# A hybrid decoder layer on one core: token projections reordered with stores in two parts, and a recurrence with two levels as rectangles

## The chip, the cores and the metric

The kernel runs on one core of one Trainium2 chip. The metric is the device time in microseconds of one execution; lower is better. Line numbers (L1153) are those of the kernel before.

## What is computed

One layer of a decoder for 1024 prompt tokens and 32 sample tokens (8 sequences of 4), all fp32: a feed-forward block, a combined projection of the normed stream, two mixers fed by it (sparse attention with an indexer that picks keys, and a gated linear recurrence), a merge, and a second feed-forward block. Two pieces matter here.

```
q, k, v, qi, ki, wi, hq, hf, hi, hg, ga, gr = split(h @ w_in)
q, k = rope(rms_norm(q)), rope(rms_norm(k));  qi, ki = rope(qi), rope(ki);  wi *= IDX_HEADS ** -0.5
# recurrence, per head (4 heads, key and value width 128)
f = lb + (1 - lb) * sigmoid(hf);  k = (1 - lb) * sigmoid(-hf);  G = cumsum(log f) within a chunk
A[t,s] = sum_d q[t,d] * exp(G[t,d] - G[s,d]) * k[s,d]   for s <= t
o = (q * exp(G)) @ S + A @ v;   S = exp(G_last) * S + (k * exp(G_last - G)).T @ v
rec = rms_norm(o) * silu(hg)
```

The projections from h, the state S of the prompt and of each sample, and the keys and values are outputs too.

## The kernel before, in words

The stages follow one another on all engines: first feed-forward (to about 832 us), token projections (834 to 1050), indexer scores, key selection with the rest of the projection, attention, recurrence (1696 to 1906), merge, second feed-forward. Each engine has its own hand-written program per stage, tied to the others by semaphores; a stage ends when SP (the queue that issues the DMAs) has seen its stores land.

**token_projections (L965 to L1336).** The columns of w_in come in seven groups of 256 (CHUNKS, L930), the last, "qk", with 72 more columns: the indexer key and the head weights. Each group is run over nine token tiles, so there are 63 steps (STEPS, L934). A step is 24 matmuls on TensorE (eight slices of depth, each as hi\*hi + hi\*lo + lo\*hi, L1153 to L1155) into one of four PSUM slots; ScalarE takes the result to SBUF (`taken`, or `out` for "hv"). Of "q" and "k" groups ScalarE squares the rows and takes a root, and VectorE does the statistics, a Newton step, the norm and the rotation (`statistics`, `norm`, `finish`); "qi" has the rotation alone; "hv" has nothing but ScalarE's copy. `finish(m)` runs one turning step late, except for "qk", where it runs at once and does the 64-wide key and the weights too, from `ki_in`, a copy that ScalarE makes (L1200). TensorE turns (transposes) the rotated rows four steps later (three for "qk", L1042), ScalarE keeps them in `stage` (L1188, L1190), and SP stores each group's `stage` whole, once its ninth tile is kept. `stage` has two slots, so a third group waits for the store of the first. The order before is: "q", then "hv" and "q" in turn, "hv" and "k", "qi" between, and last nine steps of "qk" alone. The fp32 weights come in by DMA (LOAD_AT), ScalarE makes the high part (`hi`, SPLIT_AT) and VectorE the low part (`low`, LOW_AT); TensorE waits for w_lo_done at a group's first step. In the first steps VectorE's order is: norm of step 0, `tables_with(0)` (which waits for the cosine and sine tables' DMA), step 1, then low(1). SP also fetches 64 pages of indexer keys, two a step from step 9 on.

**recurrence (L2323 to L3133).** Four heads; each head has eight prompt tiles of 128 tokens and one samples' tile, worked off in two units (u = 0: tiles 0 to 3; u = 1: tiles 4 to 8). The 128x128 lower triangle A is cut by levels: for block size b of 64, 32, 16, 8, 4, 2, 1 the later half of every 2b block looks at the earlier half, and an eighth product is the diagonal. For a level VectorE makes distances, ScalarE their exp (`decays`), VectorE the queries `qL` (`queries`); TensorE multiplies all 128 keys with 64 queries (`pair_products`, L3011 to L3024), VectorE masks the two halves (`mask`, L2872), and TensorE multiplies each level's part with the values (`outputs`, L3068, L3070). Each fp32 matmul shows as two in the trace, so eight products are sixteen. The state runs beside it: `turn` transposes the keys `kd`, ScalarE copies them to kdT, `states` multiplies with hv, VectorE updates S. Between units TensorE does outputs of the last tile, `ready` (waits for all seven `qL` of the next unit), pair_products, turn, states. Per unit VectorE also does `forget` (f from the loaded sigmoid, L2795), the scan, the masks, `variance` (L2919) and `factor` (L2944); POOL does the other steps of the norm's root (`newton`, `refine`, `gated`), the middle of which waits for `factor`.

Of the kernel before, what the change touches and what calls it, by code (L numbers as in the profile page):

```python
# [29 lines left out]
P = 128  # L30
# [892 lines left out]
HD = 64  # L923
# [6 lines left out]
CHUNKS = [("q", 0, 0), ("hv", 2632, 0), ("q", 256, 2), ("hv", 2888, CW), ("k", 512, 0), ("qi", 1024, 0), ("qk", 1280, 2)]  # L930
# [34 lines left out]
def token_projections(nc, hhi, hlo, w_in, q_gain, k_gain, cos, sin, ident, qT_d, kT_d, qiT_d, kiT_d, wi_d, hv_d,  # L965
# [10 lines left out]
    KEEP_LATER = 5  # L976
    with Scope(nc, "tok") as s:
# [3 lines left out]
        sq_room = s.sb("sq", [P, 4 * KI_COLS])  # L981
        ki_in = sq_room[:, :].rearrange("p (a b) -> p a b", b=KI_COLS)
        sq = sq_room[:, 0:CW]
        ki_out = s.sb("ki_out", [P, 2, 2 * HD + HEADS])
        taken = s.sb("taken", [P, 4, CW])
# [17 lines left out]
        ki_stored = [s.sem(f"ki_stored{n}") for n in range(2)]  # L1003
        proj_done, take_done, sq_done = s.sem("proj_done"), s.sem("take_done"), s.sem("sq_done")
# [4 lines left out]
        stage_stored = [s.sem(f"stage_stored{n}") for n in range(2)]  # L1009
        block = s.block()  # L1010
# [14 lines left out]
        def weights(w, c):  # L1025
# [3 lines left out]
            place = (c + 2) % WS  # L1029
# [10 lines left out]
        def turn_later(m):  # L1040

            return m + (3 if kind(m) == "qk" else 4)  # L1042
# [15 lines left out]
        def _(sp):  # L1058
            def load(c):
                if c > 2:  # L1060
                    sp.wait_ge(w_lo_done, c - 2)
                at = CHUNKS[c][1]
                sp.dma_start(raw[c % 2], wv[:, :, at:at + CW]).then_inc(w_loaded[c % 2], 16)
                if kind_of(c) == "qk":
                    sp.wait_ge(w_lo_done, c - 1)
                    sp.dma_start(raw[(c + 1) % 2][:, :, 0:KI_COLS], wv[:, :, at + CW:at + QK]).then_inc(w_loaded[(c + 1) % 2], 16)

            def store_stage(m):
# [4 lines left out]
                sp.dma_start(dst[b:b + 2].rearrange("b p t -> p b t"), stage[:, at, :, :]).then_inc(stage_stored[at], 16)  # L1073
                if kind(m) == "qk":
                    sp.dma_start(kiT_d[0:1].rearrange("b p t -> p b t"), stage[:, 1 - at, 0:1, :]
                                 ).then_inc(stage_stored[1 - at], 16)
# [12 lines left out]
            for m in range(M):  # L1089
                c, n = STEPS[m]  # L1090
                if m == TT:
                    sp.wait_ge(table_in, 16)
                if TT <= m < TT + DB * PAGES // 2:
                    fetch(2 * (m - TT))
                    fetch(2 * (m - TT) + 1)
                if m in LOAD_AT:
                    load(LOAD_AT[m])
                if m >= KEEP_LATER and STEPS[m - KEEP_LATER][1] == TT - 1 and turns(m - KEEP_LATER):
                    store_stage(m - KEEP_LATER)
                rows = slice(0, P) if n < TILES else slice(SROW, P)  # L1100
# [16 lines left out]
            store_stage(M - 1)  # L1117
            for slot in range(4):
                sp.wait_ge(out_stored[slot], 16 * stored_before(M, slot))
            for slot in range(2):  # L1120
                sp.wait_ge(ki_stored[slot], 32 * ((TT + 1 - slot) // 2))
            for slot in range(2):
                sp.wait_ge(stage_stored[slot], 16 * 3)
# [6 lines left out]
        def _(pe):  # L1130
# [11 lines left out]
            for m in range(M):  # L1142
# [22 lines left out]
        def _(act):  # L1165
            def hi(c):
                to = weights(whi, c)
                act.wait_ge(w_loaded[c % 2], 16 * ((c + 1) // 2))
                if kind_of(c) == "qk":
                    act.wait_ge(w_loaded[(c + 1) % 2], 16 * (c // 2 + 1))  # L1170
                    act.wait_ge(proj_done, max(STEPS.index((x, TT - 1)) for x in (c - 3, c - 4)) + 1)
                    nc.scalar.activation(to[:, :, CW:QK], raw[(c + 1) % 2][:, :, 0:KI_COLS], ACT.Copy)
                elif c >= WS:
                    act.wait_ge(proj_done, STEPS.index((c - WS, TT - 1)) + 1)
# [2461 lines left out]
```

## Time and profile before

| | us |
|---|---|
| three runs, median (lowest, highest) | 2891.18 (2888.78, 2892.44) |
| the profiled execution, own time | 2896.38 |
| its span, first to last instruction | 2894.7 |
| PE busy in it | 2793.8 (97%) |
| VectorE, ScalarE, POOL busy | 1399.2, 706.8, 572.8 |
| mean granted clock of TensorE | 0.986 |

PE's busy time is modelled, and neighbouring matmuls overlap in it, so a stage is read by start times and by windows, not by that share. In an answer of the windows view a line has the stretch, its length, then busy us and number of instructions of PE, PEld (weight load), DVE (VectorE), ACT (ScalarE) and POOL, the granted clock of TensorE (1.00 is 2.4 GHz, 0.50 is 1.2 GHz), DMA share and GB/s. A timeline line has start, length, engine, line, operation, and in brackets how long the engine had idled and what ended it. Lines of the waits view say who waited for whom, us in total, times, longest.

### The profile page before, as it was taken

Reading aid. Unit: us, or ns where it says so; the run is one execution under the profiler, and the core shown is the slowest. Engines: PE = TensorE matmul, PEld = TensorE weight load, DVE = VectorE, ACT = ScalarE, POOL = GpSimd, SP = SyncE. Lnnn points to the kernel's source line nnn. Section 1 sums busy time; section 2 is a strip of 40 time slices with the busy share of each in tenths; the row PEclk is TensorE's granted clock in tenths of the full one; section 3 lists DMA queues with packets and bytes.
Section 4 is the critical chain, followed back from the end, with each engine's and each line's share of the span. In section 5 each row is a group of like instructions: output and inputs, shape, how many; then the busy total and the mean of one; then the engine's idle time right before and its main releaser. Section 6 shows DMA issues by size and latency. Waiting matters only on the chain. (4 is left out here: it accounts for less than half of the span.)

```text
span 2894.7 us, 49785 instructions
## 1 busy us (share of the span) xinstructions
PE 2793.8 (97%) x19107; PEld 2699.3 (93%) x19107; DVE 1399.2 (48%) x2996; ACT 706.8 (24%) x1378; POOL 572.8 (20%) x384
## 2 busy tenths in 40 slices
PE   8999999999989988999989989989999999999998
PEld 7999999999979976999967879979999999999998
DVE  6223333333456637999914668756363333322223
ACT  5111111111333326122213555420231111111111
POOL 0112222111210012211232222221212211222120
PEclk9999999999999999999999999999999999999999
DMA  4111111111133130343354153244211111111101
GB/s 134 44 44 43 44 53 55 51 43 36 37 125 106 60 88 22 97 134 116 118 142 133 43 171 102 62 138 133 56 37 54 56 51 43 43 43 48 53 22 61
DMA packets 239558, 213.02 MB, mean 74 GB/s; under 512 B 27106, under 2 KB 216834, under 8 KB 239298
## 3 DMA queue, kind: packets, MB, share of 16 engines
q1 hardware_dynamic: 229122, 180.85, 21.0%
q10 hardware_dynamic: 6336, 18.88, 1.7%
q0 software_dynamic: 3968, 11.54, 1.5%
q8 instruction: 83, 1.36, 0.2%
q14 instruction: 49, 0.40, 0.0%
HBM read 168.00 MB, written 43.21 MB: 73 GB/s over the span
## 5 line engine op out<-in xcount | busy, mean ns | idle before, releaser
L639 DVE TENSOR_TENSOR ff_prod<-ff_silu,ff_gu 128x384 f32<-128x384 f32 x132 | 68.7, 521 | 795.9 <-ACT ff_silu L424 795.5
L97 PE MATMUL ff_gu<-front_hhi,over_whi 128*128 128x384 f32 (+1 forms) x1056 | 339.9, 322 | 1.0 <-DVE front_hlo L583 0.7
L97 PE MATMUL ff_gu<-rear_hhi,rear_branches 128*128 128x384 f32 (+1 forms) x1056 | 338.6, 321 | 1.2 <-DVE rear_hlo L623 1.2
L99 PE MATMUL ff_gu<-front_hhi,over_wlo 128*128 128x384 f32 (+1 forms) x1056 | 338.7, 321 | 0.0
L98 PE MATMUL ff_gu<-front_hlo,over_whi 128*128 128x384 f32 (+1 forms) x1056 | 338.6, 321 | 0.0
L98 PE MATMUL ff_gu<-rear_hlo,rear_branches 128*128 128x384 f32 (+1 forms) x1056 | 338.5, 321 | 0.0
L99 PE MATMUL ff_gu<-rear_hhi,rear_branches 128*128 128x384 f32 (+1 forms) x1056 | 338.5, 321 | 0.0
L424 ACT ACTIVATE ff_silu<-ff_gu 128x384 f32<-128x384 f32 x132 | 61.3, 465 | 859.4 <-PE ff_gu L99 859.4
L325 POOL TENSOR_TENSOR over_wlo<-over_hand,over_whi 128x1024 fp32r<-128x1024 f32 x62 | 149.1, 2427 | 580.2 <-ACT over_whi L419 579.9
L325 POOL TENSOR_TENSOR rear_branches<-ff_raw,rear_branches 128x1024 fp32r<-128x1024 f32 x62 | 149.7, 2433 | 571.0 <-ACT rear_branches L419 571.0
L97 PE MATMUL sel_proj<-front_hhi,proj_sel_whi 128*128 128x384 f32 (+1 forms) x672 | 215.5, 321 | 0.5 <-PEq L69 0.5
L98 PE MATMUL sel_proj<-front_hlo,proj_sel_whi 128*128 128x384 f32 (+1 forms) x672 | 215.5, 321 | 0.0
L99 PE MATMUL sel_proj<-front_hhi,proj_sel_wlo 128*128 128x384 f32 (+1 forms) x672 | 215.4, 321 | 0.0
L97 PEld LDWEIGHTS ff_gu<-front_hhi,over_whi 128*128 128x128 f32 x1056 | 198.2, 188 | 1.5 <-DVE over_wlo L588 1.4
L97 PEld LDWEIGHTS ff_gu<-rear_hhi,rear_branches 128*128 128x128 f32 x1056 | 198.2, 188 | 1.4 <-issue 1.4
L98 PEld LDWEIGHTS ff_gu<-front_hlo,over_whi 128*128 128x128 f32 x1056 | 198.2, 188 | 0.0
L99 PEld LDWEIGHTS ff_gu<-rear_hhi,rear_branches 128*128 128x128 f32 x1056 | 198.2, 188 | 0.0
L98 PEld LDWEIGHTS ff_gu<-rear_hlo,rear_branches 128*128 128x128 f32 x1056 | 198.2, 188 | 0.0
L99 PEld LDWEIGHTS ff_gu<-front_hhi,over_wlo 128*128 128x128 f32 x1056 | 198.2, 188 | 0.0
L652 DVE SCALAR_TENSOR_TENSOR rear_xT<-ff_dn,rear_xT 128x384 f32<-128x384 f32 (+1 forms) x264 | 136.7, 523 | 98.2 <-PE ff_dn L99 98.2
L652 DVE SCALAR_TENSOR_TENSOR x_xT<-ff_dn,x_xT 128x384 f32<-128x384 f32 (+1 forms) x264 | 136.9, 523 | 95.5 <-PE ff_dn L99 95.2
L97 PE MATMUL ff_dn<-ff_ahi,over_whi 128*128 128x384 f32 (+1 forms) x528 | 170.2, 322 | 5.5 <-DVE x_xT L652 4.3
(418 smaller groups left out, 6559.1 us busy)
## 6 DMA issues: line engine op xcount, KB each, us to landing
scratch_feat<-sel_stage ACTq DMA_DIRECT2D x32, 528.0 KB, 2.7
proj_sel_raw<-in_w_in SPq DMA_DIRECT2D x28, 512.0 KB, 3.7
over_hand<-in_ffn_w_gate SPq DMA_DIRECT2D x22, 512.0 KB, 3.8
over_hand<-in_ffn_w_up SPq DMA_DIRECT2D x22, 512.0 KB, 3.7
over_hand<-in_ffn_w_down SPq DMA_DIRECT2D x22, 512.0 KB, 3.7
ff_raw<-in_ffn_w_down SPq DMA_DIRECT2D x22, 512.0 KB, 3.3
ff_raw<-in_ffn_w_gate SPq DMA_DIRECT2D x20, 512.0 KB, 3.9
ff_raw<-in_ffn_w_up SPq DMA_DIRECT2D x20, 512.0 KB, 3.9
```

The lines of the kernel that those rows point to most:

```text
L97: nc.tensor.matmul(out, w_hi, x_hi, start=first, stop=False)
L98: nc.tensor.matmul(out, w_hi, x_lo, start=False, stop=False)
L99: return nc.tensor.matmul(out, w_lo, x_hi, start=False, stop=last)
L325: nc.gpsimd.tensor_tensor(wlo[:, u, :], raw[:, u % RAW, :], whi[:, u, :], ALU.subtract).then_inc(w_lo_done, 1)
L424: nc.scalar.activation(act_out[:, q % 2, 0:w], gu[:, q % 2, 0, 0:w], ACT.Silu).then_inc(silu_done, 1)
L639: nc.vector.tensor_tensor(prod[:, 0:w], act_out[:, b, 0:w], gu[:, b, 1, 0:w], ALU.mult).then_inc(prod_done, 1)
L652: nc.vector.scalar_tensor_tensor(x, dn[:, bank(i, j), 0:size(c)], 0.5, x, ALU.mult, ALU.add).then_inc(down_added, 1)
```

## The change

**Token projections.** The groups come in the order q, qk, q, qi, k, hv, hv: "qk" steps alternate with "q", "qi" with "q" and "k", "hv" with "k", and nine "hv" steps stand last. `low(1)` moves ahead of `tables_with(0)`. "qk" loads its 72 further columns into the other raw buffer at once. `finish` of "qk" becomes late as for the others and is turned four steps later; it reads the indexer key straight out of PSUM (ki_in and its copy go), so TensorE waits for that `finish` before it reuses the PSUM slot. Turned indexer keys go to a single 128x128 buffer `ki_stage` and are stored tile by tile; `stage` is stored in two parts, tiles 0 to 5 and 6 to 8. Page fetches begin at step 20 instead of 9, behind the step's other DMAs.

**Recurrence.** Levels 1 and 2 (b = 64 and 32) lose their full products, their masks and their output products. Three small products per prompt tile (64 keys by 64 queries, twice 32 by 32) write over those corners of the diagonal product, whose mask now keeps them. ScalarE takes log f with scale and bias from the raw input and makes `fh`, the later half of f that the level-7 queries need; `forget` goes. `variance` goes to ScalarE, `factor` to POOL. POOL's loop over heads is written out. At the end of a unit `turn` comes ahead of `ready` and `pair_products`, with four idle products (on the identity) behind it where u = 0, and ScalarE's keep_kd ahead of `logs`.

```diff
-CHUNKS = [("q", 0, 0), ("hv", 2632, 0), ("q", 256, 2), ("hv", 2888, CW), ("k", 512, 0), ("qi", 1024, 0), ("qk", 1280, 2)]
+CHUNKS = [("q", 0, 0), ("qk", 1280, 2), ("q", 256, 2), ("qi", 1024, 0), ("k", 512, 0), ("hv", 2632, 0), ("hv", 2888, CW)]
+PLACE = (2, 0, 3, 2, 0, 3, 1)
+HAD = {3: 0, 4: 1, 5: 2, 6: 1}
...
-LOAD_AT = {2: 2, 6: 3, 12: 4, 16: 5, 28: 6}
-SPLIT_AT = {0: 1, 6: 2, 11: 3, 18: 4, 24: 5, 41: 6}
-LOW_AT = {2: 1, 8: 2, 13: 3, 20: 4, 26: 5, 43: 6}
+LOAD_AT = {1: 2, 3: 3, 11: 4, 18: 5, 26: 6}
+SPLIT_AT = {0: 1, 7: 2, 14: 3, 22: 4, 32: 5, 42: 6}
+LOW_AT = {9: 2, 16: 3, 24: 4, 34: 5, 44: 6}
...
-                if c > 2:
-                    sp.wait_ge(w_lo_done, c - 2)
+                if c > 1:
+                    sp.wait_ge(w_lo_done, max(c - 2, 1))
...
+                cols, sem = (slice(0, FIRST * P), stage_stored) if STEPS[m][1] < TT - 1 else (slice(FIRST * P, T), rest_stored)
+                sp.dma_start(dst[b:b + 2].rearrange("b p t -> p b t")[:, :, cols], stage[:, at, :, cols]).then_inc(sem[at], 16)
+
+            def store_ki(m):
+                n = STEPS[m][1]
+                sp.wait_ge(kept_done, turns_through(m))
+                to = slice(n * P, (n + 1) * P) if n < TILES else slice(SEQ, T)
+                sp.dma_start(kiT_d[0][:, to], ki_stage[:, 0:to.stop - to.start]).then_inc(ki_stage_stored, 16)
...
                 if m >= 4:
                     pe.wait_ge(take_done, m - 3)
+                    if kind(m - 4) == "qk":
+                        pe.wait_ge(out_done, turns_through(m - 4))
...
                 if kind(m) == "qk":
-                    last = nc.scalar.activation(stage[:, 1 - at % 2, 0, to], turned[:, x, 2, cols], ACT.Copy)
+                    if n:
+                        act.wait_ge(ki_stage_stored, 16 * n)
+                    last = nc.scalar.activation(ki_stage[:, 0:cols.stop - cols.start], turned[:, x, 2, cols], ACT.Copy)
...
-                    if kind(m) == "qk":
-                        nc.scalar.activation(ki_in[:, m % 4, :], proj[:, m % 4, CW:QK], ACT.Copy)
...
                     if m == 0:
+                        low(1)
                         tables_with(0)
...
-                if kind(m) == "qk":
-                    finish(m)
-                    waiting = None
...
-            levels = range(1, 5) if x == 0 else range(5 if n < TILES else NL - 2, NL)
+            levels = range(MASKED_FROM, NL - 2) if x == 0 else range(NL - 2, NL)
...
+            return [(y, at, LEVELS[y - 1]) for y in range(1, MASKED_FROM) for at in range(0, P, 2 * LEVELS[y - 1])]
...
+                pool.wait_ge(multiplied, 2 * V + 2)
+                nc.gpsimd.tensor_scalar(tmp[:, 0:w], tmp[:, 0:w], -0.5, 1.5, ALU.mult, ALU.add).then_inc(factor_ready, 1)
...
-                act.wait_ge(f_ready, U + 1)
-                nc.scalar.activation(logf[:, COLS[u]], f[:, COLS[u]], ACT.Ln).then_inc(log_ready, 1)
+                act.wait_ge(f_loaded[u], 16 * h + 16)
+                nc.scalar.activation(logf[:, COLS[u]], f[:, COLS[u]], ACT.Ln, scale=omlb[:, DynSlice(h, 1)],
+                                     bias=lb[:, DynSlice(h, 1)]).then_inc(log_ready, 1)
+                wait(act, qL_ready, (NL - 1) * (U - 1))
+                nc.scalar.activation(fh[:, side_by_side(NL - 1, u)], half(f[:, span(NL - 1, u)], NL - 1, 1), ACT.Identity,
+                                     scale=omlb[:, DynSlice(h, 1)], bias=lb[:, DynSlice(h, 1)]).then_inc(f_ready, 1)
...
+                nc.scalar.activation(v, total, ACT.Identity, scale=1.0 / P, bias=eps[:, 0:1]).then_inc(var_ready, 1)
...
+                    if x and n < TILES:
+                        for y, at, b in rectangles():
+                            q_at = n * HD + at // 2
+                            last = nc.tensor.matmul(pairs[at:at + b, i % RING, lo + at + b:lo + at + 2 * b],
+                                                    kL[:, y - 1, n * P + at:n * P + at + b], qL[:, y - 1, q_at:q_at + b],
+                                                    start=True, stop=True)
...
                     if nxt and last:
+                        pe.wait_ge(decay_ready, (LATE + 1) * (2 * after[0] + after[1]) + 1)
+                        turn(*nxt)
+                        if u == 0:
+                            idle_products(nc, pairs[:, 3, 0:P], ident, 4)
                         ready(*after)
                         pair_products(*nxt)
-                        turn(*nxt)
```

## Rows read from the trace of the kernel before

**Rows 1.** the windows view: stretch, length, busy us (x instructions) per engine, PE clock

```profile
834.10:845.80 11.70, 11.70 (x96) 11.54 (x96) 3.27 (x11) 4.78 (x7) 0.00 (x0) 1.00 0.71 235
845.80:851.40 5.60, 0.04 (x1) 0.00 (x0) 5.29 (x15) 0.89 (x3) 0.00 (x0) 0.88 0.01 3
851.40:857.40 6.00, 5.97 (x30) 5.98 (x31) 5.49 (x24) 1.22 (x5) 0.00 (x0) 0.54 0.00 0
857.40:1004.20 146.80, 146.80 (x1238) 146.80 (x1236) 92.83 (x322) 50.18 (x131) 0.00 (x0) 1.00 0.28 83
1004.20:1044.60 40.40, 35.82 (x244) 34.97 (x241) 18.02 (x71) 7.56 (x31) 0.00 (x0) 1.00 0.18 61
...
1823.20:1836.80 13.60, 13.19 (x57) 12.11 (x58) 6.55 (x16) 5.37 (x16) 1.33 (x1) 0.51 0.32 102
```

**Rows 2.** waits of PE in 834 to 1060 us: total, times, longest

```profile
PE tok_proj L1153 <- DVE tok_wlo L1236: 5.6, 1, 5.6
PE tok_turned L1137 <- ACT tok_stage L1190: 3.9, 2, 3.2
```

**Rows 3.** timeline of ACT and DVE, 839 to 850 us

```profile
839.50 1.90 ACT L1175 ACTIVATE tok_whi<-tok_raw 128x2048 fp32r<-128x2048 f32 x1
...
844.37 0.76 DVE L1249 TENSOR_TENSOR tok_cs_gain<-tok_cs,tok_gains 128x576 f32<-128x576 f32 x1 [3.53 <-DMA tok_sn<-in_t_sin]
...
849.08 2.29 DVE L1236 TENSOR_TENSOR tok_wlo<-tok_raw,tok_whi 128x2048 fp32r<-128x2048 f32 x1
```

**Rows 4.** timeline at the end of the projections; last row: DMA view, landing

```profile
1044.82 0.38 ACT L1201 ACTIVATE tok_taken<-tok_proj 128x256 f32<-128x256 f32 x1
...
1055.90 3.68 PE L1476 MATMUL idx_turned<-core_ident,fetch_idx_pages 128*64 128x128 f32 x32 [6.34 <-PEq L69]
...
scratch_hv<-over_hand SPq DMA_DIRECT2D x16, 128.0 KB, 1.8
```

**Rows 5.** timeline of DVE, two normed steps and one step with indexer keys

```profile
851.29 0.41 DVE L1277 TENSOR_REDUCE tok_var<-tok_sq 128x4 f32<-128x256 f32 x1
...
854.47 0.42 DVE L1277 TENSOR_REDUCE tok_var<-tok_sq 128x4 f32<-128x256 f32 x1
...
1046.19 0.29 DVE L1261 TENSOR_TENSOR tok_rb<-tok_taken,tok_sn 128x128 f32<-128x128 f32 x1
...
1047.52 0.19 DVE L1261 TENSOR_TENSOR tok_rb<-tok_sq,tok_sn 128x32 f32<-128x32 f32 x1
...
1048.37 0.17 DVE L1314 TENSOR_SCALAR tok_ki_out<-tok_sq 128x8 f32<-128x8 f32 x1
```

**Rows 6.** timeline of PE in the recurrence, one prompt tile and the samples' tile

```profile
1785.90 1.67 PE L3023 MATMUL hg_pairs<-hg_qL,hg_kL 128*128 128x64 f32 x14
...
1794.15 0.30 PE L3023 MATMUL hg_pairs<-hg_qL,hg_kL 128*32 128x16 f32 x4
1794.30 0.23 PE L3023 MATMUL hg_pairs<-hg_q,hg_kL 128*32 128x32 f32 x2
1794.46 0.49 PE L3059 MATMUL hg_o_ps<-hg_q_in,hg_S 128*128 128x128 f32 x2
```

**Rows 7.** timeline of PE where one half unit of a head ends

```profile
1776.92 0.44 PE L3068 MATMUL hg_o_ps<-hg_attn,hg_hv 128*128 128x128 f32 x2
1778.09 1.77 PE L3023 MATMUL hg_pairs<-hg_qL,hg_kL 128*128 128x64 f32 x14 [0.72 <-DVE hg_qL L2854]
...
1779.97 0.27 PE L3031 MATMUL hg_turned<-core_ident,hg_kd 128*128 128x128 f32 x1
1780.66 0.46 PE L3040 MATMUL hg_turned<-hg_hv,hg_kdT 128*128 128x128 f32 x2 [0.41 <-issue]
```

**Rows 8.** waits of PE in 1700 to 1915 us

```profile
PE hg_pairs L3023 <- DVE hg_qL L2854: 1.7, 3, 0.7
```

**Rows 9.** timeline of DVE and POOL, 1816 to 1823 us

```profile
1818.13 1.40 POOL L2600 TENSOR_TENSOR hg_sq<-hg_sq,hg_var 128x544 f32<-128x544 f32 x1
1818.25 1.57 DVE L2854 TENSOR_TENSOR hg_qL<-hg_q,hg_f 128x272 f32<-128x272 f32 x1
```

More of the change, by code:

```diff
@@ L976, in token_projections @@
     KEEP_LATER = 5
+    FIRST = 6
+    FETCH_AT = 20
     with Scope(nc, "tok") as s:
@@ L1009, in token_projections @@
         stage_stored = [s.sem(f"stage_stored{n}") for n in range(2)]
+        rest_stored = [s.sem(f"rest_stored{n}") for n in range(2)]
         block = s.block()
@@ L1321, in _ @@
                 if not turns(m):
+                    if waiting is not None and not any(turns(x) for x in range(m, M)):
+                        finish(waiting)
+                        waiting = None
                     continue
@@ L2501, in load_f @@
             def load_f(h, u):
-                wait(sp, qL_ready, (NL - 1) * (2 * h + u - 1))
+                wait(sp, f_ready, 2 * h + u - 1)
+                wait(sp, log_ready, 2 * h + u - 1)
                 feat(8, h, u, f, f_loaded)
@@ L2626, in _ @@
             load_first(pool)
-            heads(pool, unit)
+            heads_one_by_one(unit)
             pool.wait_ge(gate_loaded[1], 16 * HG)
@@ L2738, in unit @@
                         decays(*after, (2, 3, 4, 5))
+                    if before and j == 1:
+                        variance(*before)
                     if before and j == 2:
@@ L2751, in unit @@
                         end_square(n - TILES + 1)
+                    if nxt and last:
+                        keep_kd(*nxt)
                     if beyond and last:
                         logs(*beyond)
-                    if nxt and last:
-                        keep_kd(*nxt)
             act.wait_ge(bound_ready, 2)
             act.wait_ge(tiny_set, 1)
+            act.wait_ge(eps_set, 1)
             logs(0, 0)
@@ L2964, in unit @@
                         distances(*after, (0, 2, 3))
-                    if before and j == 1:
-                        variance(*before)
                     if after and j == 1:
@@ L2970, in unit @@
                         queries(*after, (2, 3, 4))
-                    if before and j == 3:
-                        factor(*before)
                     if u == 1 and j == 3:
                         decayed_states(h)
-                    if beyond and last:
-                        forget(*beyond)
                     if after and j == 3:
@@ L2995, in unit @@
                         scan(*beyond)
-            forget(0, 0)
             scan(0, 0)
@@ L3001, in _ @@
             queries(0, 0, (*range(2, LATE + 1), LATE + 1, 1))
-            forget(0, 1)
             mask(0, 0)
@@ L3069, in outputs @@
                         else:
-                            last = nc.tensor.matmul(half(o, y, 1), hv[:, n, :], blocks(part, y), start=False, stop=(n == 0 and y == 1))
+                            last = nc.tensor.matmul(half(o, y, 1), hv[:, n, :], blocks(part, y), start=False, stop=(n == 0 and y == MASKED_FROM))
                 if n == TILES:
@@ L3602, in shape_tables @@
     s_, t_ = row[:, None], row[None, :]
-    levels = np.concatenate([((s_ // (2 * b) == t_ // (2 * b)) & (s_ % (2 * b) < b))[:, row[row % (2 * b) >= b]] for b in LEVELS]
-                            + [s_ == t_], 1)
+    within = [(s_ // (2 * b) == t_ // (2 * b)) & (s_ % (2 * b) < b) & (t_ % (2 * b) >= b) for b in LEVELS]
+    levels = np.concatenate([m[:, row[row % (2 * b) >= b]] for m, b in zip(within[2:], LEVELS[2:])]
+                            + [(s_ == t_) | within[0] | within[1]], 1)
     return {"t_cos": cos, "t_sin": sin, "t_ident": np.eye(P),
```

99 lines of the change are left out of this document (47 added, 52 removed).

## The prediction

> **What bounds the kernel now.** The page shows PE busy at 97%, so time is won only where PE waits, where it runs at half its clock, or where it has less to do. Two stages are touched. I read first the windows view, cut where PE's stream breaks, then the waits of PE, then timelines around each break.
>
> In the token projections (834.10 to 1055.90, where the next stage's first matmul starts, 221.8 us) PE has three losses. At 845.80 it has done four steps and stands still for 5.6 us [rows 1] for the low part of the second group's weights [rows 2]. That part, made at 849.08, stood behind the tables, which began only at 844.37, when their DMA landed, though ScalarE had the high part ready at 841.4 [rows 3]. From 851.4 PE is granted 0.54 for 6.0 us [rows 1], half clock, after having done nothing for 5.6 us: 3.0 us more lost. In the last nine steps (1004.20 to 1044.60) PE is busy for 35.82 of 40.40 us [rows 1]: 4.6 us of waits, most of it for the copy of turned indexer keys into a stage buffer whose store was late [rows 2]. Then come 11.3 us from the last projection to the next stage [rows 1, 4]: four tiles to turn, keep and store.
>
> In the recurrence PE goes tile by tile without a stop, about 4.1 us per prompt tile. It stops only at the ends of units: for queries at the ends of u = 0 (1.7 us in three waits, [rows 7, 8]) and in the wait for kdT behind the late turn: 1779.97 to 1780.66 is 0.69 us where one transpose's pace is 0.11, so 0.58 us lost [rows 7]. From 1823.20 PE is at 0.51 for 13.6 us [rows 1]: 6.7 us lost, behind one of those ends.
>
> **The change, part by part.** The sum is made against the profiled execution; its own time, 2896.4, is 5.2 us above the median of the runs, which I carry at the end.
>
> *Token projections.* PE's matmuls and transposes stay the same. Its pure work is 11.7 + 3.0 (6.0 us at half clock) + 146.8 + 35.8, and 1.4 for twelve transposes at 0.12 (146.80/1238, [rows 1]) that stood behind the last step: 198.7 us.
> - low(1) ahead of the tables: the high part now has 72 further columns, and their load (288 KB) ahead of the tables. The high part was ready at 841.4 [rows 3]; with a third more bytes in flight and a quarter more columns I put it at 843.3, the low part (2.29 us in [rows 3], and 0.75, an estimate by columns) at 846.3. PE wants it at 845.8. So 0.5 us of waiting instead of 5.6, and no half clock. The tables follow at 846.3 to 847.8; all normed steps start some 2 us later on VectorE.
> - "qk" between "q": VectorE needs 3.18 us for a normed step [rows 5]. For "qk" it needs 1.33 (1046.19 to 1047.52) and 1.02 (1047.52 to the end of the row at 1048.37) [rows 5], some 2.5 with synchronisation. A pair is 5.7 us. PE needs 2.93 for the normed step (11.70/4, [rows 1]), 35.82/9 = 4.0 for "qk" with its transposes, and 0.24 for two more: 7.2 us. VectorE keeps up, with 1.5 us to spare per pair, minus low(2) and low(3), 2.3 each. But it starts late: three normed steps from 847.8 end at 857.4, finish of step 3 (1.35) at 858.8, statistics of step 5 (0.7) at 859.5, and finish of the first "qk" step (step 4) at 862.0. PE has to wait for it before step 8, and has done steps 4 to 7, with eight transposes, at 846.3 + 2 x 3.6 + 2 x 2.9 + 8 x 0.12 = 860.3. That new wait is 1.7 us. Behind it the next finish comes 5.7 later and PE 7 later. I add 0.8 for close places: 3 us of waits in all, bounds 0.5 and 8.
> - SP: the loads of groups 2 and 3 now stand at steps 1 and 3 and wait for w_lo_done(1), 846.3; behind them nothing is due before step 4's stores, and such a load, issued as the stage began, was in use 5.4 us later [rows 3]; steps 7 and 14 split them. Each "qk" step issues three DMAs (key, weights, turned tile) where SP waits for finish of that step; the turned tile of step m-5 goes behind them, and ScalarE's next keep waits for it, because ki_stage is single. By my times keep(6) waits some 1.5 us, while PE is still in a step of 4.1: hidden; without that cover 1.5 us a pair. The stage stores in two parts lift the wait for a store of [rows 2]. The page fetches stay two a step, only from step 20 on and behind the step's stores; nothing in this stage waits for them. POOL's queue is empty here.
> - The end: the last nine steps ask nothing of VectorE. From the last matmul: 0.25 to ScalarE, 0.38 copy [rows 4], 0.1 and 1.8 for the hv store to land [rows 4], 0.8 to the next stage: 3.3, I take 3.5 for 11.3.
> New stage: 198.7 + 3.0 + 3.5 = 205.2, against 221.8: **-16.6 us**. Bounds by the waits 0.5 to 8, and by a clock that falls in the last gap (up to 1 us at the next stage): -11 to -19.
>
> *Recurrence, rectangles.* A full pass of a product has a pace of 0.107 us ((1.67 - 0.28)/13, [rows 6]). Two levels go in pair_products and in outputs: 8 passes, -0.86 us a tile. Three rectangles of two passes come. With 32 columns of weights a pass takes 0.0375 (1794.15 to 1794.30 is four), and going from such a tile back to full ones costs 0.085 (1794.30 to 1794.46 less two passes) [rows 6]. With 64 columns no row has it: bounds 0.0375 and 0.107, I take 0.07, between the two widths. So 2 x 0.07 + 4 x 0.0375 = 0.29, and three changes of shape (full to 64, 64 to 32, back) at 0.08: 0.53 a tile, bounds 0.31 and 1.12 (every pass at the full pace, every change at twice the row). Net -0.33 x 32 tiles = -10.5 us, bounds -17.6 and +8.3. Masks shrink by 64 columns each; VectorE is not what PE waits for there.
> The row shows a change of shape at 0.085 us. By the Trainium skill, TensorEngine Tiling (Array Packing), Key Properties, a change of tiling mode drains TensorE, whatever the tile; if a drain were the 0.28 of a matmul less its pace, 0.17, the tile would be 0.27 dearer and the gain 1.9 instead of 10.5; the row speaks for the smaller price.
>
> *Turn ahead of the products.* At seven unit ends the 0.58 goes: **-4.0 us**. It now waits for the next unit's first decays, made three tiles earlier: nothing. Queued behind it are only PE's own idle products.
> *Idle products.* Eight passes at four ends, at 0.12 about 1.0 us an end: +4.0 us. They fill the waits for queries: -1.7.
> *VectorE, ScalarE, POOL.* `forget`, `variance` and `factor` leave VectorE, three operations a unit; ScalarE gets `variance` and `fh`, by columns some three copies of 0.38 [rows 4], 1.1 us a unit, beside four tiles of 3.8 us each. If it did not hide, keep_kd at the second tile is late by up to 0.7 us, seven times. POOL's factor shortens the hand-over between its own steps. I cost these at nothing; what they do is keep the queries as early as PE now comes. Should they not, the wait at u = 0 ends is late next.
> Sum: -10.5 - 4.0 + 4.0 - 1.7 = **-12.2 us**.
>
> *Half clock at 1823.* It followed the unit end at 1822.8, where PE waited; idle products now stand there. I expect it gone in the profile: -6.7. But the profiled run is 5.2 us above the median, and I cannot tell whether every run had that stretch, so against the median I take half, **-3.4**.
>
> Total: 16.6 + 12.2 + 3.4 = 32.2 us; 2891.2 - 32.2 = **2859.0 us**. A difference under 0.2% (5.8 us) could not be told from none.
>
> **Rivals.**
> 1. *Cheaper.* Rectangles cost the lower bound (0.31) and the half clock was in every run: 7.0 + 3.3 more, 2849. For it: small passes at 0.0375. Against: nothing shows 64 columns. 18%.
> 2. *VectorE late all through the qk pairs*, so that waits are 8 us or more, not 3: 2865 to 2868. For it: pair times of 5.7 and 7.2 leave 13 us over nine pairs, of which 4.6 goes for low parts, and a late start must be worked off too. Against: the first waits give it time. 12%.
> 3. *POOL holds VectorE.* The query of 1818.25 took 1.57 us under a POOL product of 1.40 that ended with it [rows 9]. Factor on POOL adds such a stretch, 1.0 to 1.4 us, once a unit; at the three u = 0 ends with a norm it may delay the last query: +3 to +4, 2863. The Trainium skill (SBUF — State Buffer, SBUF: two separate sides) has a lock on a port pair that a GpSimd op and a VectorE op with two SBUF inputs take in turn; the trace agrees. 9%.
> 4. *Full price rectangles*, 1.12 a tile: +19, 2878. 4%.
> 5. *Slower.* Each of the six small passes runs alone for its whole 0.28 us and each change costs its row: 1.68 + 0.26 = 1.94 a tile, +1.41 x 32 = 45 us, 2904. It decides from 1.53 a tile on, where it eats the 32. For it: their output positions differ (0 and 64), which no row has; against: [rows 6]. 3%.
>
> **The numbers.** Forecast 54% (own range 2852 to 2866), rivals 18, 12, 9, 4, 3. Range for eight in ten: 2846 to 2872, leaving out rivals 4 and 5 and the tails. Faster by over 0.2% (under 2885.4): 0.96; within: 0.01; slower: 0.03.
>
> **What would show it.** Windows: the stage from 834 to its next stage in about 205 us, no half clock near 850, one wait of about 2 us of tok_proj for tok_ki_out near 860, tail 3.5. In the recurrence a prompt tile of 3.75 us instead of 4.08, kdT not waited for at unit ends, no half clock inside. Wrong if a tile takes 4.1 or more, or if waits for VectorE repeat each pair of "qk".

## The result, and the profile after

The changed kernel takes 2870.88 us (median of 7 runs, 2867.09 to 2872.32), the kernel before 2891.18 beside it; the ratio is 0.9914, with a 95% interval of 0.9898 to 0.993. So 20.3 us were won. The forecast was 2859.0, a gain of 32.2. The time lies at the upper end of the range (2846 to 2872), 1.1 us inside it: the gain in the token projections fell outside the bounds given to it, and the early turn, which had none, brought little.

The profiled execution took 2872.32 us with a span of 2870.2, 24.5 us less than before. It divides so (first and last starts of PE's rows in both traces; "half clock" is half the length of the stretches where the clock records show 1.2 GHz instead of 2.4, and less than that is lost where PE stands still in such a stretch):

| part | before | after | difference | half clock before, after |
|---|---|---|---|---|
| up to the token projections | 834.1 | 832.0 | -2.1 | 0, 1.7 |
| projections to the next stage's first matmul | 221.8 | 215.0 | -6.8 (forecast -16.6) | 7.3, 6.8 |
| on to the recurrence's first product | 658.0 | 652.6 | -5.4 (forecast 0) | 21.7, 17.1 |
| first product to last product group | 175.6 | 162.9 | -12.7 (forecast -18.9) | 6.8, 0 |
| the rest | 1005.2 | 1007.7 | +2.5 (forecast 0) | 5.1, 11.8 |

The windows view of the changed kernel, cut where PE's stream breaks (stretch, length, busy us and instructions of PE, PEld, DVE, ACT, POOL, granted clock, DMA share, GB/s):

```profile
832.00:845.50 13.50, 13.23 (x96) 13.04 (x96) 4.82 (x11) 5.46 (x8) 0.00 (x0) 0.87 0.50 149
845.50:856.30 10.80, 10.76 (x76) 10.51 (x76) 9.98 (x39) 2.96 (x10) 0.00 (x0) 1.00 0.60 196
856.30:859.10 2.80, 0.05 (x2) 0.01 (x1) 2.66 (x11) 0.55 (x3) 0.00 (x0) 1.00 0.00 0
859.10:863.50 4.40, 4.40 (x25) 4.40 (x26) 3.79 (x16) 0.48 (x2) 0.00 (x0) 0.61 0.05 8
...
916.00:920.00 4.00, 0.07 (x2) 0.01 (x1) 3.16 (x14) 0.34 (x2) 0.00 (x0) 0.76 0.70 259
920.00:924.90 4.90, 4.90 (x23) 4.90 (x24) 0.00 (x0) 2.28 (x3) 0.00 (x0) 0.50 0.17 40
...
1004.00:1044.50 40.50, 40.50 (x340) 40.31 (x339) 5.05 (x20) 6.72 (x20) 0.00 (x0) 1.00 0.28 90
1699.50:1871.90 172.40, 167.32 (x1400) 149.16 (x1398) 119.96 (x276) 101.11 (x293) 44.64 (x36) 1.00 0.35 111
```

What was removed is gone. The second group's low part is waited for 0.3 us instead of 5.6 [rows 1, 2]; the last nine steps run without a stop; the recurrence has a full clock from end to end, where [rows 1] has 13.6 us at 0.51. But two stops with nothing in them are new, at 856.3 and at 916, and half clock stands behind each. The waits of PE between 840 and 1045 us:

```profile
PE tok_turned L1148 <- ACT tok_stage L1200: 3.9, 2, 2.8
PE tok_turned L1148 <- ACT tok_ki_stage L1204: 3.9, 1, 3.9
PE tok_proj L1166 <- DVE over_wlo L1250: 0.3, 1, 0.3
```

**The stop at 856.3** is for ScalarE's copy of a turned tile. ScalarE and VectorE there (start, duration, line, operation, idle time before it and its releaser):

```profile
858.34 0.18 DVE L1291 RECIPROCAL tok_inv<-tok_var 128x4 f32<-128x4 f32 x1
...
858.55 0.20 ACT L1226 ACTIVATE tok_root<-tok_inv 128x4 f32<-128x4 f32 x1 [3.19 <-DVE tok_inv L1291]
858.67 0.37 ACT L1200 ACTIVATE tok_stage<-tok_turned 128x256 f32<-128x256 f32 x1
```

The tile to be copied had long been turned. ScalarE stood 3.19 us in the wait for step 5's statistics, and the copy was queued behind that root.

**The stop at 916** is for the single buffer ki_stage. SP's queue, then ScalarE:

```profile
911.07 0.43 SPq L1068 DMA_DIRECT2D tok_raw<-in_w_in  x1
911.54 0.58 SPq L1078 DMA_DIRECT2D scratch_qiT<-tok_stage  x1
912.17 0.47 SPq L1084 DMA_DIRECT2D scratch_kiT<-tok_ki_stage  x1
...
919.66 0.28 ACT L1204 ACTIVATE tok_ki_stage<-tok_turned 128x128 f32<-128x128 f32 x1 [4.44 <-DMA scratch_kiT<-tok_ki_stage]
```

The DMA view of 900 to 925 us (KB each, median us from issue to landing):

```profile
tok_raw<-in_w_in SPq DMA_DIRECT2D x1, 1024.0 KB, 6.4
scratch_qiT<-tok_stage SPq DMA_DIRECT2D x1, 768.0 KB, 7.9
scratch_kiT<-tok_ki_stage SPq DMA_DIRECT2D x3, 64.0 KB, 1.6
```

The store of 64 KB takes 1.6 to 1.8 us as a rule (median 1.8 over the nine) and took 7.5 here (912.17 to 919.66), behind the load of 1 MB and the store of 768 KB. The Trainium skill says (DMA: Bandwidth & Descriptors, Queues, rings and completion order) that each DMA engine takes up one queue's descriptors in order and that the completion increment lands behind every earlier write of that engine; the trace agrees.

**In the recurrence** a prompt tile takes 3.82 us instead of 4.08 [rows 6] (1769.26 and 1773.08 are the starts of two tiles). PE there, and the second tile of a u = 0 unit with ScalarE beside it:

```profile
1773.08 1.23 PE L3038 MATMUL hg_pairs<-hg_qL,hg_kL 128*128 128x64 f32 x10
1774.14 0.44 PE L3038 MATMUL hg_pairs<-hg_q,hg_kL 128*128 128x128 f32 x2
1774.51 0.51 PE L3043 MATMUL hg_pairs<-hg_qL,hg_kL 128*64 128x64 f32 x6
1774.96 0.49 PE L3080 MATMUL hg_o_ps<-hg_q_in,hg_S 128*128 128x128 f32 x2
1775.28 0.78 PE L3091 MATMUL hg_o_ps<-hg_attn,hg_hv 128*128 128x64 f32 x6
...
1748.14 0.28 PE L3052 MATMUL hg_turned<-core_ident,hg_kd 128*128 128x128 f32 x1
...
1749.87 0.49 PE L3061 MATMUL hg_turned<-hg_hv,hg_kdT 128*128 128x128 f32 x2 [0.83 <-ACT hg_kdT L2760]
```

```profile
1747.56 0.73 ACT L2681 ACTIVATE hg_kL<-hg_k_in,hg_omlb 128x544 f32<-128x544 f32 x1
1748.26 0.23 ACT L2702 ACTIVATE hg_kd<-hg_kd 128x32 f32<-128x32 f32 x1
1748.39 1.26 ACT L2705 ACTIVATE hg_kd<-hg_kk,hg_G 128x128 f32<-128x128 f32 x4
1749.56 0.25 ACT L2760 ACTIVATE hg_kdT<-hg_turned 128x128 f32<-128x128 f32 x1
```

kdT isn't waited for at unit ends any more; it is waited for one tile later, seven times, 4.3 us in all. Six of the seven are new: the first unit's is in the kernel before too, alone there:

```profile
1720.52 0.49 PE L3040 MATMUL hg_turned<-hg_hv,hg_kdT 128*128 128x128 f32 x2 [0.89 <-ACT hg_kdT L2721]
```

In the changed kernel's second tile the transpose was done at 1748.4, but the copy stood behind kL and the next unit's decayed keys until 1749.56.

### The profile page after: what moved, and what is told of

The parts are those of the page before. It is cut to its first block and busy times, and to the rows that moved or that the text cites. A ratio compares the mean times of both kernels' runs of the same rounds, so it can differ in the third digit from the quotient of the medians.

```text
span 2870.2 us, 49741 instructions
## 1 busy us (share of the span) xinstructions
PE 2785.1 (97%) x19075; PEld 2687.0 (94%) x19075; DVE 1382.6 (48%) x2975; ACT 713.6 (25%) x1384; POOL 576.5 (20%) x391
```

## The experiments

The ratios are against the kernel before on the same chip; its median was 2891 to 2897 us from job to job, so the medians of different jobs are compared through it. The profiles settle what is below the noise: "stage" is from the first tok_proj to the next stage's first matmul, "recurrence" from the first to the last start of the products (162.9 us in the changed kernel, 175.6 before). Each is one profile: where the projections are those of the changed kernel (e1, e3, e4, e7 to e10 and itself), the stage takes 212.9 to 215.0 us.

**1. The two halves alone.** e1 is the kernel before with the diff's parts up to line 1350, e2 with those of the recurrence and its masks.

> The token projections of the changed kernel with the recurrence of the kernel before. Theory (the token part brought about half of what was forecast, because three new waits of PE of 2.75, 3.93 and 1.19 us and half clock behind two of them stand in the place of the old 5.6 and 4.6 us): the stage takes about 215 us from its first matmul to that of the next stage, the three waits are there again, and the median falls by 7 to 11 us. Rival (the forecast of 16.6 us holds for this part by itself, and it is together with the new recurrence that something is lost): 15 to 19 us.

> The recurrence of the changed kernel behind the token projections of before. Theory: prompt tile 3.82 us for 4.08, a wait for kdT at the second tile of seven units (4.3 us in all), no half clock inside the recurrence; from the first hg_pairs to the last hg_o_ps 172 us for 185.5, and a median lower by 9 to 14 us, the width being whether the half clock at 1823 was in every run. Rival (the forecast for this part, 15.6 us, holds and all of the shortfall lies in the tokens): 15 us or more. Rival (half clock comes back elsewhere in the recurrence): 6 to 7 us.

e1: 2889.24 us (12 runs), ratio 0.9986 (0.997 to 1.0001). e2: 2880.4, ratio 0.996 (0.9944 to 0.9976).

```profile
PE tok_turned L1148 <- ACT tok_ki_stage L1204: 3.8, 1, 3.8
PE tok_turned L1148 <- ACT tok_stage L1200: 3.4, 2, 2.2
```

These are e1's waits: the same stops at the same places, and a stage of 213.7 us. e2's stage, with the projections of before, took 221.1, though its wait for the low part was 2.2 us and not 5.6. So the old loss there depends on when the loads land (in e2 the tables' work began at 842.40, before at 844.37), and the tokens bring 6 to 9 us of stage in these traces. e1's median shows less than was expected, 4 us against its control, with an interval that just includes none, and its profile has more time at half clock, most of the excess behind the recurrence (97.6 us of it in the whole span, 82.0 in the profile of before); whether that belongs to the change isn't settled. The rival, the forecast's 16.6 us for this part, is refuted. e2's recurrence took 162.8 us, the changed kernel's time, and e1's 175.6 with the 13.7 us of half clock (at 1813 there): that stretch belongs to the old recurrence, in both profiles that have it.

**2. What the rectangles bring.** e3 sets MASKED_FROM = 1, e4 sets it to 2, with HALF_AT and the masks to match:

```diff
-    MASKED_FROM = 3
-    HALF_AT = (0, 3 * HD)
+    MASKED_FROM = 1
+    HALF_AT = (0, 5 * HD)
```

> The changed kernel with levels 1 and 2 as full masked products again (no rectangle; everything else of the change stays). Theory: a rectangle block costs 0.60 us a tile where eight full passes cost 0.86, so the prompt tile is 4.08 us for 3.82 and the run 8 us longer than the changed kernel, some 12 us below the kernel before. Rival (the forecast): 10.5 us longer. Rival (the shape changes drain PE so that the rectangles bring hardly anything, and what the recurrence won is the turn and the clock): 2 us or less longer.

> The changed kernel with level 1 alone (one rectangle of 64 x 64, two passes) as a rectangle and level 2 as a full masked product. It tells the passes from the changes of shape. Theory A (going to small passes and back costs 0.19 us whatever their number, a pass 0.07): prompt tile 3.98 us. Theory B (each change of size costs, 64 to 32 too, and the passes themselves are nearer 0.05): 3.93 us. Theory C (passes at the full pace of 0.107, changes cheap): 4.0 us or more.

e3: 2878.58 us, ratio 0.9946 (0.9928 to 0.9965). Its tile is 4.08 us, its recurrence 168.9, so the rectangles are worth 6.0 us there, not the 10.5 of the forecast. 0.26 a tile would be 8.3. Part of the rest is lost where kdT is waited for: from a u = 0 unit's first products to those of its third tile both kernels take the same 7.76 us (1743.35 to 1751.11, in e3 1750.03 to 1757.79). Where all of the missing 2.3 us went isn't settled. Through the controls e3's median is some 9 us above the changed kernel's. e4 (a single run, 2872.18) has a tile of 4.09 us, as theory C has it and neither A nor B: one rectangle in the place of four full passes brings nothing. PE in e4's tile:

```profile
1775.07 0.44 PE L3038 MATMUL hg_pairs<-hg_q,hg_kL 128*128 128x128 f32 x2
1775.44 0.33 PE L3043 MATMUL hg_pairs<-hg_qL,hg_kL 128*64 128x64 f32 x2
1775.70 0.49 PE L3080 MATMUL hg_o_ps<-hg_q_in,hg_S 128*128 128x128 f32 x2
```

From the starts of single instructions: the last full pass begins at 1775.23 and the first of 64 columns 0.205 us later, where a full pass has a pace of 0.11: 0.09 for the way in. The second of 64 columns comes 0.107 later, no faster than a full one. After it, 0.15 to the next full pass, and that one has no weights loaded ahead, 0.21 instead of 0.11 (1775.70 to 1775.91). In all about 0.45 us for two passes, against 0.43 for the four that went. So C was right on the pace and wrong on the changes, which aren't cheap. The changed kernel adds four passes of 32 columns, whose starts are 0.007, 0.046 and 0.007 us apart: about 0.18 us with the step from 64 to 32, again against 0.43. That is where its 0.26 comes from.

**3. The load behind the small store.** e5:

```diff
-LOAD_AT = {1: 2, 3: 3, 11: 4, 18: 5, 26: 6}
+LOAD_AT = {1: 2, 3: 3, 11: 4, 19: 5, 26: 6}
```

> The changed kernel with the load of the sixth group's weights issued one step later, behind the store of the indexer key's turned tile instead of ahead of it. Theory (that 32 KB store landed 7.5 us after its issue because a load of 1 MB stood 1.1 us ahead of it in the queue, ScalarE waited for it with the next copy, and PE with a transpose): PE's wait of 3.9 us at 920 goes and the half clock of 6.8 us behind it too; the stage falls from 215 to about 208 us, the median by 4 to 7 us. Rival (the store is late through the page fetches that follow, or through the single buffer itself): the wait stays over 2 us and the median within 1.

2866.44 us, ratio 0.9906 (0.9891 to 0.9921). SP and ScalarE in e5:

```profile
911.69 0.43 SPq L1078 DMA_DIRECT2D scratch_qiT<-tok_stage  x1
912.16 0.47 SPq L1084 DMA_DIRECT2D scratch_kiT<-tok_ki_stage  x1
912.67 0.96 SPq L1068 DMA_DIRECT2D tok_raw<-in_w_in  x1
...
915.84 0.28 ACT L1204 ACTIVATE tok_ki_stage<-tok_turned 128x128 f32<-128x128 f32 x1
```

The store is issued at the same time and lands after 3.8 us at the most, still behind the store of 768 KB but not the load; PE has no wait there, no half clock behind, and the stage is 208.0 us. The theory holds in the trace (the 32 KB of its text are 64): 7.0 us below the changed kernel for one number, of which 0.8 lies in the two earlier waits (3.4 and 0 for 3.9 and 0.3), which e4 has as short without this edit; 4.9 to 7.0 below the eight profiles named above. The median, against its control, is only some 2 us better than the changed kernel's, and the intervals overlap.

**4. The copy ahead of the root.** e6, in ScalarE's loop of the token projections:

```diff
+                for x in range(M):
+                    if turns(x) and turn_later(x) + 1 == m:
+                        keep(x)
                 if normed(m):
...
                     nc.scalar.activation(root[:, :], inv[:, :], ACT.Sqrt).then_inc(root_done, 1)
-                for x in range(M):
-                    if turns(x) and turn_later(x) + 1 == m:
-                        keep(x)
```

> The changed kernel with ScalarE's copy of the turned tile ahead of the square and root of the same step. Theory (PE's wait of 2.2 to 2.8 us at 859 is for a copy that stands behind a root, which waits for VectorE's statistics; the same at 967): both waits change, the first to one for the finish of the first step with indexer keys, 1.3 us at most, the second goes; stage 2 to 3 us shorter, and with the half clock behind the first wait gone up to 4.5. Rival (VectorE is late there whatever ScalarE's order is): the sum of PE's waits in the stage falls by less than 1 us.

2870.99 us, ratio 0.9915 (0.99 to 0.993), no difference from the changed kernel. The waits of PE, 840 to 1045:

```profile
PE tok_turned L1148 <- ACT tok_ki_stage L1204: 6.7, 2, 6.0
PE tok_proj L1166 <- DVE over_wlo L1250: 1.8, 1, 1.8
PE tok_proj L1166 <- DVE tok_ki_out L1326: 1.1, 1, 1.1
```

The mechanism is right: the waits for tok_stage at 859 and 967 are gone, and the first became 1.1 us for tok_ki_out, the very wait that the forecast had put at step 8. But PE only comes earlier to the store at 916, which lands when it did, and waits 6.0 us for it instead of 3.9. The waits in the stage sum to 9.6 us for 8.1 (1.5 of that is the low part, which varies from run to run), not 2 to 3 us less, and the stage, 213.1 us, is inside the spread of the unrepaired ones.

**5. Decayed keys behind the copy of kdT.** e7, in ScalarE's unit loop:

```diff
                     if after and j == 0:
                         total_decay(*after)
                         scaled_keys(*after)
-                        decays(*after, (0,))
...
                     if nxt and not last:
                         keep_kd(*nxt)
+                    if after and j == 0:
+                        decays(*after, (0,))
```

> The changed kernel with ScalarE's four decayed keys (kd) of the next unit behind the copy of kdT instead of ahead of it, at the second tile of a unit. Theory (the copy of kdT is late there because ScalarE is 0.5 us behind, and four activations of 0.32 us stand before it): PE's seven waits for kdT, 4.3 us in all, shrink under 0.5 us in all, nothing else gets late, and the run is 4 us shorter. Rival (ScalarE is full at that place and only hands the delay on): the waits for kdT go but others of 2 us or more come, at the unit ends or for decays and queries; net under 1 us.

2867.88 us, ratio 0.9904 (0.9888 to 0.992). The copy now follows its transpose at once:

```profile
1749.96 0.28 PE L3053 MATMUL hg_turned<-core_ident,hg_kd 128*128 128x128 f32 x1
...
1750.69 0.44 PE L3062 MATMUL hg_turned<-hg_hv,hg_kdT 128*128 128x128 f32 x2
```

```profile
1750.27 0.28 ACT L2760 ACTIVATE hg_kdT<-hg_turned 128x128 f32<-128x128 f32 x1 [0.17 <-PE hg_turned L3053]
1750.45 0.22 ACT L2702 ACTIVATE hg_kd<-hg_kd 128x32 f32<-128x32 f32 x1
1750.57 1.26 ACT L2705 ACTIVATE hg_kd<-hg_kk,hg_G 128x128 f32<-128x128 f32 x4
```

None of the seven waits is left, no other came, and the recurrence takes 157.0 us: 5.9 less, more than the 4.3 that the waits view counts. The view counts from the modelled end of the last matmul, and start to start the difference is larger (the second tile at u = 0 went from 5.57 to 4.52 us, 1.05 for a wait of 0.83; at u = 1 0.56 for 0.30). The median is some 3 us better than the changed kernel's through the controls, with intervals that overlap.

**6. Idle products, and the turn.** e8, and below it e9, which also puts ScalarE's copy of kdT behind `logs` again:

```diff
                         turn(*nxt)
-                        if u == 0:
-                            idle_products(nc, pairs[:, 3, 0:P], ident, 4)
                         ready(*after)
```

```diff
-                        pe.wait_ge(decay_ready, (LATE + 1) * (2 * after[0] + after[1]) + 1)
-                        turn(*nxt)
...
                         ready(*after)
                         pair_products(*nxt)
+                        turn(*nxt)
```

> The changed kernel without the eight added passes at the four u = 0 ends. Theory (they cost 3.6 us; without them PE would wait there for queries, as before, 0.4 to 0.7 us each, and the half clock of 13.7 us that both kernels with the old recurrence had behind the third such end comes back): net 1 to 5 us longer. Rival (the half clock went because the waits are shorter by themselves, with the lighter VectorE): 2 to 3.6 us shorter, no half clock between 1700 and 1870.

> The changed kernel with the transposes of kd at unit ends behind the products again, and the copy of kdT behind the logs, as before; the idle products stay. Theory (the forecast's term): a wait for kdT of 0.58 us comes back at seven unit ends, 4 us, and no half clock, since without the wait for queries it stands alone: the recurrence 4 us longer than 162.9. Rival (the early turn is what removed the half clock of 13.7 us, since the run without idle products did not have it either): 10 to 11 us longer.

e8: 2873.06 us, ratio 0.993 (0.9916 to 0.9944). e9: 2874.68, ratio 0.9915 (0.9893 to 0.9936). The waits of PE in the recurrence, e8 and then e9:

```profile
PE hg_turned L3061 <- ACT hg_kdT L2760: 4.3, 7, 0.9
PE hg_pairs L3038 <- DVE hg_qL L2892: 2.5, 4, 0.7
```

```profile
PE hg_turned L3061 <- issue: 2.9, 7, 0.4
PE hg_turned L3061 <- ACT hg_kdT L2760: 0.9, 1, 0.9
```

e8's recurrence takes 162.7 us: PE waits 2.5 us for queries in the place of the products, so they cost and bring nothing, as far as the recurrence goes. The median moved up by some 5 us through the controls, which its profile, taken in its fastest run, doesn't show; that stays open. e9's takes 165.5, of which 1.7 is a half clock after the first unit, so 163.8: the early turn is worth 0.9 us, neither the 4 of the theory nor the 10 of the rival. It took the wait from the unit's end and gave it back at the second tile; in e9, as before, the view has one there in the first unit alone, 0.9 us. Neither kernel has the half clock of 13.7 us back. (e9's seven "issue" waits of 2.9 us in all are those at unit ends, as in [rows 7].) In the old recurrence queries and kdT are waited for 2.6 us apart [rows 7], and the stretch came at one of three such ends; with one of the two waits gone, whichever, it wasn't. That fits both runs, and e3's too, but no run put both waits into the new kernel, so it is not shown.

**7. Further levels, and the repairs together.** e10 sets MASKED_FROM = 4 (four rectangles of 16 x 16 for level 3 too). With it the output of the prompt's recurrence is wrong, for a reason that isn't known, so e10 and e12 show what these instructions take and not what a right kernel would. e11 is e5, e6 and e7 together, e12 is e11 with e10.

> The changed kernel with level 3 as rectangles too (four of 16 x 16, eight passes, in the place of four full passes). Theory (what costs is the way to small passes and back, 0.09 and 0.23 us, paid already; a small pass then has a pace of some 0.03): 0.25 us for 0.43, prompt tile 3.64 us for 3.82, run 3 to 6 us shorter. Rival (a further change of size costs 0.09 and passes of 16 columns are no cheaper than 0.0375): tile 3.78, run within 1.5 us.

> The changed kernel with the load of the sixth group later, ScalarE's copy of the turned tile first, and the decayed keys behind the copy of kdT. Theory (the gains of the three add, and with the load out of the way the second brings its own): stage 205 to 206 us for 215, recurrence 157 for 162.9, the run 14 to 17 us below the changed kernel. Rival (what one repair gives the other had already, or half clock comes elsewhere): 10 us or less below.

> The three repairs and level 3 as rectangles. Theory (PE is what bounds the recurrence, so the shorter tile adds wholly: 0.18 us x 32): 5 to 6 us below the run with the three repairs, recurrence 151 us. Rival (VectorE and ScalarE are late for the shorter tiles, and waits for queries or decays take the place): recurrence 155 us or more.

| | median | ratio | stage | recurrence | tile |
|---|---|---|---|---|---|
| e10 | 2868.9 | 0.9885 (0.9865 to 0.9904) | 214.1 | 157.5 | 3.42 |
| e11 | 2859.05 | 0.9865 (0.9845 to 0.9885) | 208.6 | 157.0 | 3.82 |
| e12 | 2853.47 | 0.9836 (0.9816 to 0.9856) | 211.3 | 148.8 | 3.42, 3.62, 3.77 |

```profile
1799.83 0.55 PE L3043 MATMUL hg_pairs<-hg_qL,hg_kL 128*64 128x64 f32 x14
1800.31 0.49 PE L3080 MATMUL hg_o_ps<-hg_q_in,hg_S 128*128 128x128 f32 x2
```

In e10 fourteen passes take 0.48 us to the next full one, where six took 0.44 (1774.51 to 1774.96): the eight small ones cost 0.04 for 0.43 saved. Both theories had them too dear. e10's waits for kdT grew to 7.3 us. e12, with the repair, has a recurrence 8.2 us shorter than e11's, more than the theory's 6, but not the 0.4 us for each of 32 tiles, 12.8, that the tile would give: most units have a tile of 3.62 or 3.77 us, and 0.8 us of waits for queries are back. The rival isn't met, but what it describes has begun.

e11 is the fastest that computes the whole layer. Its span makes it 13.3 us shorter than the changed kernel (2856.9 to 2870.2), just short of the 14 to 17 expected. The recurrence did what was expected, the stage did not: 208.6, where e5 alone had 208.0.

```profile
PE tok_turned L1148 <- ACT tok_ki_stage L1204: 3.8, 2, 2.3
...
PE tok_proj L1166 <- DVE tok_ki_out L1326: 1.1, 1, 1.1
```

What the first copies gained is waited for at the single buffer again, twice, at 915 and 924. The second time the store takes 1.6 us to land, but SP issued it only at 922.22, behind two page fetches that had held its queue from 920.66; the forecast said that nothing in this stage would wait for them. A second ki_stage wasn't tried.

## Why the prediction was right, and where it was not

Right were the direction, the range, and the places where time was to be won. That the range held, by 1.1 us, is in part luck. The forecast's own range, 2852 to 2866, was missed: the projections brought 6.8 us for 16.6 and the recurrence 5.9 for 12.2, and the half clock, counted at half, came in whole and made up for 3.4. The room above 2866 was there for a rival, a VectorE late all through the pairs, that didn't happen. Point by point:

- *low(1) ahead of the tables.* 0.5 us forecast, 0.3 measured (0 to 1.8 over the runs with this part), and full clock from 845.5 on.
- *"qk" between "q", waits of 3 us in all.* Mis-sized: 3.9, not counting the store's. The step failed that said PE "has to wait for it before step 8", for VectorE's finish. VectorE's lateness reached PE sooner, by way of ScalarE: its copy of a turned tile is queued behind a root, and the root waits for VectorE. 2.75 us for 1.7, and once more 1.19 at 967 (e6 removed both, and the forecast wait came out at 1.1). That VectorE keeps up with the pairs after that was right: there is no wait for it in pair after pair, so rival 2 did not happen.
- *SP.* The step failed that called keep(6)'s wait for ki_stage "hidden". The forecast counted what SP's queue holds back at the issue, 1.5 us, and not what the DMAs ahead in that queue do to the landing: 7.5 us behind 1 MB. 3.9 us of waiting and 2.4 of half clock (4.9 us at 0.50 once PE ran again); e5's stage is 7.0 shorter, 0.8 of it elsewhere.
- *Half clock.* None was forecast in the stage, 6.8 us came by the table's count, 1.7 of it as the stage begins (e2, with the projections of before, has that too). PE stood still for 1.9 us of the stretch at 918, so 5.9 us were lost. PE fell to 1.2 GHz behind both new stops, as it had near 850 behind the old one. The bounds of the stage, -11 to -19, allow for it in the last gap alone; measured is -6.8: 5.2 us more of waits, 5.9 of half clock, 1.0 less for the end and 0.3 for the pure work. Removing a stop took its half clock along, but a new stop can bring one, and the sum has to carry both together.
- *The end.* 2.5 us from the last matmul (1044.5 to 1047.0) for 3.5; right, and the stage store in two parts with it.
- *Rectangles.* -10.5 forecast, -6.0 in e3. Passes of 64 columns went in at 0.07 and cost 0.107, the upper bound. The four of 32 columns went in at 0.15 and cost about 0.1. The way in cost 0.09, the step between 0.04 and the way back 0.09 at the first full pass and 0.10 more at the second, 0.3 us together beside the forecast's 0.24; the row that gave 0.085 shows the first part of the way back alone. The whole block was 0.60 against 0.53. The drain by the Trainium skill (TensorEngine Tiling (Array Packing), Key Properties) is seen in these changes; as a price of 0.17 for each it would have made the tile's gain 0.06, and the trace gives 0.26: the three changes cost some 0.1 each, nearer the row's 0.085 than 0.17.
- *Turn ahead of the products, -4.0.* 0.9 in e9. Failed is the step "VectorE, ScalarE, POOL ... I cost these at nothing". The text named the case, keep_kd late at the second tile by 0.7, seven times, and gave it no chance of its own. It came at six places, 0.5 us late at u = 1 and 1.0 at u = 0 (from transpose to product, against e7), and took back 3.1 of the 4.0 us (e9). Putting the copy first (e7) is worth more than that, 5.9 us, because it also removes what was late already: 1.1 us in the first unit, and 0.3 in each of the other u = 0 units, which e9 has too. Earlier at a unit's end, PE is as much earlier at the second tile, where ScalarE still stands in six activations for the next unit. The added work was low too: fh takes 0.62 us and variance 0.69 (L2673, L2741), 1.3 a unit and not 1.1.
- *Idle products.* +4.0 and -1.7 forecast, +0.2 in e8.
- *Half clock at 1823.* 6.8 us gone, as forecast for the profile. e1 has the stretch as well, so both profiles with the old recurrence have it, and counting it at half was too little for them; what the unprofiled runs had isn't on record.
- *POOL.* Its factor took 0.72 us, not 1.0 to 1.4, and no wait of PE for queries is left in the changed kernel inside the recurrence. Rivals 1, 3, 4 and 5 did not happen. What the lighter VectorE is worth by itself wasn't tried.

The terms with their measured sizes: 6.8 us in the projections, 5.9 in the recurrence (12.7 less the half clock) and 6.8 of half clock, 19.5 us, where the forecast had 16.6, 12.2 and 3.4, 32.2. The medians give 20.3. The other parts of the span, 5.0 us shorter in sum, are about what the profiled run of before lay above its median (5.2); half clock between the two stages alone was worth 8.5 to 21.7 us in the profiles of this study, in kernels that are the same there.

## What to carry to other kernels

When a stall is taken away, PE reaches the next hand-over earlier by the same amount. Walk on from there to the next instruction that takes something from each other engine, and read what that engine has queued ahead of it: an in-order queue makes a copy as late as the unrelated wait ahead of it. For a small DMA that frees a single buffer, count the bytes issued just ahead of it in its queue, not its own; issuing one load one step later was worth as much stage time as the rest of that part of the change. A change of shape on PE is paid once for the group, so small passes pay by number: two of 64 columns brought nothing, four more of 32 brought 0.26 us a tile. (They are narrower too; no run tells the number from the width.)

## What the hardware did that was not expected

Passes of few columns with different output positions run side by side, as far as starts show it: the four 32-column passes, at positions 0 and 64, start in pairs 0.007 us apart, and in e10 some of the 16-column passes start ahead of 32-column ones that stand before them in the program, and the eight cost 0.04 us together, where a full pass costs 0.107. The Trainium skill has this (TensorEngine Tiling (Array Packing), Key Properties: tiles are independent and can load weights and multiply in parallel). A 64-column pass alone at one position is no cheaper than a full one.

A wait costs PE more than the view counts for it, since the view starts from a modelled end: seven waits of 4.3 us in sum were worth 5.9 when they went.

Half clock mostly follows a stop closely and in the same places from run to run: behind the stops at 859 and 916 in the changed kernel, in e1, e3 and e4 alike, and with the stop at 916 gone in e5, not there. Not always as long: e7 and e8 have 3.4 us for 6.8 behind the second stop, and e9, with the same stop at 859, has none behind it.
